# A hybrid decoder layer with expert retrieval: the projections and the convolution done per group of tokens, and two blocks instead of one summed on VectorE

## What is computed

```python
h = rmsnorm(x, norm1_g)
z_glu, q, k, v, qm, gate_logits = jnp.split(h @ w_in, IN_SPLITS, axis=-1)
conv_y = silu(layernorm(depthwise_conv31(a * sigmoid(b)))) @ w_conv_out   # a, b: halves of z_glu
swa_o  = sliding-window attention over blocks of 128; mem_o = attention over 256 memory tokens
merged = g_conv * conv_y + g_swa * (swa_o @ w_swa_out) + g_mem * (mem_o @ w_mem_out)
x = x + merged @ w_out
xb = rmsnorm(x, norm2_g)                  # then, for every block of 128 tokens:
eid, gate = top-16 of 128 x 128 product keys, for each of 8 heads      # 128 experts per token
act = gelu(einsum('td,thkd->thk', xb, w_down[eid]))
x = x + einsum('thk,thkd->td', gate * act, w_up[eid])
```

## Time and profile before

| | |
|---|---|
| time, median of 3 runs | 3336.84 us (3334.49 to 3349.33) |
| span of the profiled execution | 3347.1 us |
| TensorE busy | 3087.0 us, 92% |
| VectorE busy | 2512.8 us, 75% |
| GpSimd busy | 1611.7 us, 48% |
| ScalarE busy | 779.2 us, 23% |
| moved by DMA | 1077.16 MB, mean 322 GB/s |

### The profile page before, as it was taken

How to read it: one execution, slowest core, us unless ns; L and a number is a source line. 1 busy time by engine, 2 the same in 40 slices (tenths; PEclk the granted TensorE clock), 3 DMA queues, 4 the chain that set the end, 5 groups by cost and what they waited for, 6 DMA issues and landing times.

```text
span 3347.1 us, 33154 instructions
## 1 busy us (share of the span) xinstructions
PE 3087.0 (92%) x11349; PEld 1818.7 (54%) x11349; DVE 2512.8 (75%) x5082; ACT 779.2 (23%) x2063; POOL 1611.7 (48%) x1269
## 2 busy tenths in 40 slices
PE   8999798998989999779999999999999999997874
PEld 5677687866847654445545445545545545543321
DVE  2298434986889789888988888888888868455556
ACT  2001542321310114324214204204204214200000
POOL 0000002545145677745566667557657657444434
PEclk9999899999998999899999999999999999998998
DMA  3111466999599999999999999999999999899998
GB/s 130 43 37 58 147 204 231 336 334 354 197 339 351 359 404 397 331 368 370 381 353 388 357 380 388 344 389 385 358 377 380 359 400 373 335 410 393 408 410 316
DMA packets 326171, 1077.16 MB, mean 322 GB/s; under 512 B 40468, under 2 KB 73877, under 8 KB 325340
## 3 DMA queue, kind: packets, MB, share of 16 engines
q0 software_dynamic: 172416, 625.03, 48.7%
q1 hardware_dynamic: 119275, 428.87, 34.1%
q10 hardware_dynamic: 34312, 21.16, 2.0%
HBM read 1052.50 MB, written 23.94 MB: 322 GB/s over the span
## 4 chain that ended last, share of the span: by engine, by line
PE 29%; DMA 20%; DVE 15%; issue 13%; POOL 10%; ACT 1%; ACTq 1%; DVEq 0%; POOLq 0%
PE psum L1666 17%; DMA arena<-in_w_down,arena 12%; POOL arena L1404 9%; DMA arena<-in_w_up,arena 7%; DVE arena L2019 5%; PE psum L1469 4%; PE psum L1642 2%; PE psum L1529 2%; PE psum L1513 1%; ACTq L2264 1%; PE psum L1612 1%; DVE arena L2113 1%; DMA arena<-scratch_s 1%; DMA arena<-in_w_q 1%; PE psum L1515 1%
## 5 line engine op out<-in xcount | busy, mean ns | idle before, releaser
L1404 POOL DMA_INDIRECT arena<-in_w_down,arena x1024 | 1419.2, 1386 | 735.5 <-DVE arena L2019 503.1
L1666 PE MATMUL psum<-arena 128*128 128x512 f32 x3584 | 1602.0, 598 | 77.1 <-DMA arena<-in_w_up 70.8
L2019 DVE CUSTOM_DVE_ANT_0 arena<-arena 128x1024 f32<-128x1024 f32 x1024 | 1220.0, 1222 | 256.3 <-DMA arena<-in_w_down,arena 247.8
L1666 PEld LDWEIGHTS psum<-arena 128*128 128x128 f32 x3584 | 664.4, 191 | 871.0 <-issue 734.3
L1513 PE MATMUL psum<-arena 128*128 128x256 f32 (+2 forms) x1536 | 361.6, 390 | 17.0 <-DVEq L1831 5.5
L2321 ACT ACTIVATE arena<-arena 128x128 f32<-128x128 f32 x896 | 285.6, 390 | 323.8 <-DVE arena L2043 314.7
L2043 DVE TENSOR_TENSOR arena<-constants,arena 128x1024 f32<-128x1024 f32 x224 | 273.4, 1224 | 77.7 <-PE psum L1469 65.0
L1513 PEld LDWEIGHTS psum<-arena 128*128 128x128 f32 x1536 | 267.9, 195 | 99.5 <-issue 13.3
L1469 PEld LDWEIGHTS psum<-arena 128*128 128x128 f32 x1792 | 237.8, 195 | 153.2 <-ACT arena L2321 86.6
L1469 PE MATMUL psum<-arena 128*128 128x128 f32 x1792 | 245.0, 281 | 40.4 <-ACT arena L2321 40.2
L2113 DVE SCALAR_TENSOR_TENSOR arena<-arena 128x1024 f32<-128x1024 f32 x128 | 164.4, 1284 | 122.6 <-DMA arena<-in_w_up,arena 121.3
(11 more groups left out here) (317 smaller groups left out, 2039.8 us busy)
## 6 DMA issues: line engine op xcount, KB each, us to landing
arena<-in_w_up SPq DMA_DIRECT2D x512, 512.0 KB
arena<-in_w_gates SPq DMA_DIRECT2D x96, 768.0 KB
arena<-in_w_o SPq DMA_DIRECT2D x40, 512.0 KB
arena<-in_w_q SPq DMA_DIRECT2D x32, 512.0 KB
arena<-in_w_down,arena POOLq DMA_INDIRECT x1024
arena<-in_w_chunks SPq DMA_DIRECT2D x26, 512.0 KB, 3.5
arena<-scratch_s POOLq DMA_DIRECT2D x64, 128.0 KB
scratch_s<-arena ACTq DMA_DIRECT2D x11, 512.0 KB
```

The costliest lines, as they stand in the source:

```text
L1404: pool.indirect_dma_start(dst, None, table, bass.IndirectOffsetOnAxis(ap=idN[:, min(n, NT - 1) % 2, j:j + 1], axis=0)).then_inc(here, 16)
L1666: mm = pe.matmul(psum[:, 2 * (m % 2) + h, :], coef_block(m, s % NKEYS), wup[s % WUPR][:, h * 512:(h + 1) * 512], start=first, stop=end)
L2019: dve.tensor_tensor_reduce(row, row, rowD[slot_of["x", n]], 1.0, 0.0, ALU.mult, ALU.add, dots[:, n % 3, j:j + 1]).then_inc(row_used, 1)
```

## The change

The first program block now normalises the first 128 columns, then the rest, then the memory, and multiplies nothing but the sums of squares. The 26 chunks become items of the third block, for each group of columns anew, with their weights in the ring of three buffers: per group four "ba" (both halves of the gated unit, two chunks each), four "qq" (queries, two chunks each), one "kv", and once four "mm" (memory, two chunks each). That makes 4 x 9 x 2 + 8 = 80 chunk loads. The convolution is done per group in eight parts on VectorE, the normalisation behind it per group ("ls", "lv"). The planner places all of them. GB = 2 blocks are summed on VectorE, DENSE is 6, so that (6 + 1) x 64 = 448 pieces of w_up are read and 2 x 128 up rows gathered.

```diff
+        FIRST_LOADS = [("b", 0), ("a", 0), ("b", 1)]
...
-        DENSE = NT - 1
+        GB = 2
+        DENSE = NT - GB
...
-        items = att(0) + mixed(pairs_of(0, 0)[0:6], range(1, 6), 1) + pairs_of(0, 0)[6:] + mixed(pairs_of(0, 1, 2), range(6, 10), 4)
...
+        items = glus(0) + [("kv", 0)] + qi[0:2] + [("bu", 0), ("bu", 1)] + mems[0:2] + st[0] + qi[2:3] + st[1] + [("mt",)] + qi[3:4]
+        items += st[2] + [("ls", 0)] + mems[2:3] + st[3] + [("lv", 0)] + mems[3:4] + st[4] + \
+            pairs_of(0, 0)[0:2] + st[5] + pairs_of(0, 0)[2:]
+        items += woven_in(pairs_of(0, 1, 2), {8: glus(1)[0:1], 12: glus(1)[1:2]})
+        for a in (1, 2, 3):
+            bs, qi, qs, st = glus(a), heads_in(a), queries(a - 1), att_steps(a)
+            old_us = group_us[a - 1]
+            items += outs(a - 1, 0) + bs[2:3] + turns(old_us[0:1]) + bs[3:4] + turns(old_us[1:2]) + qs[0:1] + [("kv", a)] + qs[1:4] + scores(old_us)
...
+            items += qi[0:2] + st[0] + qi[2:3] + st[1] + qi[3:4] + st[2] + [("ls", a)] + st[3] + [("lv", a)] + st[4] + st[5]
...
+                items += mixed(pr, st[6:], 1) + woven_in(pairs_of(a, 1, 2), {8: glus(a + 1)[0:1], 12: glus(a + 1)[1:2]})
...
-        rows_at = [48704, 49728, 50752, 11328, 37888] + [25600 + D * i for i in range(4)] + [46144] + [8256 + D * i for i in range(3)] + \
+        rows_at = [48704, 49728, 50752, 33792, 34816] + [25600 + D * i for i in range(4)] + [46144] + [8256 + D * i for i in range(3)] + \
...
-        open_from = [0] * 5 + [184] * 4 + [KEPT] + [122] * 3 + [2] + [80] * 2 + [0] * 2 + [190] * 2
-        open_to = [SLOTS * (NT + 1)] * 3 + [262, 116] + [SLOTS * (NT + 1)] * 5 + [262] * 3 + \
-            [310] + [258] * 2 + [50] * 2 + [238, 258]
+        open_from = [0] * 5 + [350] * 4 + [KEPT] + [310] * 3 + [2] + [80] * 2 + [0] * 2 + [205] * 2
+        open_to = [UPS] + [SLOTS * (NT - 1) + 96] * 2 + [15, 15] + [UPS] * 5 + [370] * 3 + \
+            [390] + [370] * 2 + [50] * 2 + [350, 370]
...
+        accs = [rowD[q] for q in SUM_SLOTS]
...
+            if convs and conv_due <= m.now and all(m.done("glu", item_of("ba", 2 * (convs[0][1] // 4) + c, convs[0][0])) for c in range(2)):
+                m.put("conv", *convs.pop(0))
+                conv_due = m.now + (4.0 if convs and convs[0][0] else 0.0)
+                continue
...
+                    elif it[0] in ("ba", "qq"):
+                        first, n = group_cols(it[2])
+                        for j in range(2):
+                            w = load_here(k, j)
+                            for c in range(KD):
+                                mm = pe.matmul(psum[:, b + j, 0:n], w[:, c, :], hT[:, c, first:first + n],
+                                               start=(c == 0), stop=(c == KD - 1))
+                        mm.then_inc(item_done, 1)
...
                 def up(u):
-                    if u == 0:
-                        dve.wait_ge(coef_done, NT)
-                        dve.wait_ge(x1last_here, 16)
-                    else:
+                    g, j = u // SLOTS, u % SLOTS
+                    if j == 0:
+                        dve.wait_ge(coef_done, DENSE + g + 1)
+                        dve.wait_ge(x1last_here[g], 16)
+                    if u:
                         dve.wait_ge(up_sum, u)
                     row = row_wait(("up", u))
-                    dve.scalar_tensor_tensor(out=acc, in0=row, scalar=dots[:, (NT - 1) % 3, u:u + 1],
-                                             in1=acc if u else x1last, op0=ALU.mult, op1=ALU.add).then_inc(up_sum, 1)
+                    dve.scalar_tensor_tensor(out=accs[g], in0=row, scalar=dots[:, (DENSE + g) % 3, j:j + 1],
+                                             in1=accs[g], op0=ALU.mult, op1=ALU.add).then_inc(up_sum, 1)
...
+                def conv(a, part):
+                    first, n = conv_cols(a)
+                    half, q = part // 4, part % 4
...
+                    for t in range(8 * q, min(8 * q + 8, TAPS)):
+                        for c in (2 * half, 2 * half + 1):
+                            y = yT[:, c, first:first + n]
...
+                                ins = dve.scalar_tensor_tensor(out=y, in0=uT[:, c, t:t + n], scalar=cw[:, c, t:t + 1], in1=y,
+                                                               op0=ALU.mult, op1=ALU.add)
```

More of the change, by code:

```diff
@@ L311, in _ @@
+                mm.then_inc(summed, 1)
+                for k in range(KD):
+                    pe.wait_ge(squared, 2 * KD + k + 1)
+                    mm = pe.matmul(psum[:, 3, 0:MEM], ones, sqm[:, k, :], start=(k == 0), stop=(k == KD - 1))
+                mm.then_inc(summed, 1)
             @block.vector
@@ L448, in build_kernel @@
+        probT = [memN[:, i // 4, (i % 4) * P:(i % 4 + 1) * P] for i in range(8)]
         ck = at(29120, NB, WIN + 1)
@@ L555, in build_kernel, with glus, heads_in, woven_in @@
-        items += pr[4:5] + qs[2:3] + [("xv",)] + qs[3:4] + scores([3, 4]) + pr[5:] + pairs_of(3, 1, 2)[0:12] + [("ids0",)] + pairs_of(3, 1, 2)[12:]
+        def glus(a):
+            return [("ba", c, a) for c in range(NC)]
+        def heads_in(a):
+            return [("qq", i, a) for i in range(NC)]
+        def woven_in(main, extra):
+            out = []
+            for i, it in enumerate(main):
+                out += extra.get(i, []) + [it]
+            return out
+        mems = [("mm", i) for i in range(NC)]
@@ L1075, in build_kernel @@
             if sample_att < 3 and m.landed.get(("load", SAMPLE_LOADS), m.now) + 4.0 <= m.now:
-                ready = [True, m.done("item", items.index(("xs",))), m.end.get(("xmax",), m.now) + 2.5 <= m.now][sample_att]
+                ready = [m.done("copied", last_ao), m.done("item", items.index(("xs",))), m.end.get(("xmax",), m.now) + 2.5 <= m.now][sample_att]
                 if ready:
@@ L1099, in build_kernel @@
                 continue
-            if dot_next == SLOTS * (NT + 1) and not last_put and m.end["up", SLOTS - 1] + 3.0 <= m.now:
-                m.put("last")
-                last_put = True
+            if last_next < GB and m.end.get(("up", SLOTS * last_next + SLOTS - 1), m.now) + 4.0 <= m.now:
+                m.put("last", last_next)
+                last_next += 1
                 continue
@@ L1221, in rec_index @@
             return NX + recs.index(s) + 1
+        tail = [s for s in plan if s[0] in ("snorm", "last") or s in (("norm", DENSE - 2), ("norm", DENSE - 1))]
         row_order = [s for s in plan if s[0] in ("dot", "up")]
```

878 lines of the change are left out of this document (516 added, 362 removed).

## The result

The changed kernel takes 3524.39 us (median of 4 runs, 3519.83 to 3528.24), the kernel before, run beside it, 3342.53 (4 runs, 3334.49 to 3349.33): ratio 1.0537, 95% interval 1.0511 to 1.0563. It is slower by 5.4%. The forecast was 3373 us, slower by 1.1%, with a range up to 3475. The side was right, the size was not: 151 us are missing. (The kernel before was run again beside the experiments, with medians of 3346.76 us beside e1 to e4, 3352.64 beside e5 to e8, 3350.22 beside e9 to e11 and 3347.60 beside e12. A difference between runs of two such groups can carry up to 10 us of that, and where it matters the ratios to the kernel before are compared.)

The account below looks back on a forecast made before the run. A queue of bytes that starts late: dense steps start at 1544 us with 470 gathers done, 692 MB at 380 GB/s take 1821 us, plus 18: 3383 us span, 3373 in the median's terms (+1.1%); range 3250 to 3475.

Parts of the forecast that it names:

- end = T + 2487 - 1.38 R: Whole kernel: end in the profiled span's terms from T and R; the span stood 10 us over the median.
- T: Time at which the dense steps start: 1459 us before, 1544 us forecast, bounds 1474 to 1635.
- R: Number of gathers done by T: 377 before, 470 forecast, bounds 415 and 540.
- The largest term, 60 us of waits for in_w_chunks: Before the dense steps: 40 two-chunk items wait on a ring of three buffers, +60 us, bounds 0 and 121.
- My reading through the planner's tables: Gathers done by T from rows the new table demands: 317 + 80 + 60 = 457.
- the one through VectorE's time: Gathers done by T from VectorE 92% busy between 360 us and T: near 470.
- After T: From the dense steps' start: 692 MB at 380 GB/s take 1821 us, then 18 us to the end.
- TensorE's freed 264 us at nothing: Behind T: TensorE saves 229 us of records and 35 of scatter products, but ends nothing sooner.
- the one on the last gathers: End of kernel: GpSimd issues last gathers 1.32 us apart, under the 1.38 that 0.524 MB take at 380 GB/s.
- Items wait: Rival, slower still: two-chunk items wait 3.02 us each, 3433 us; lone last gathers may add 52 us; chance 0.17.
- lone gathers are slow: Sign of being wrong: DMA share well below 0.95 after T, from this or another bound.
- The rule that spoke against the last step: Last gathers: two-port VectorE instructions lock GpSimd out of writing descriptors, so adds would stretch each gather; the trace doesn't show it.

Follow-up runs that it names:

- e1: The changed kernel with one block, not two, left to fetched up rows, seven multiplied, the group-wise front kept: 3380.21 us, ratio 1.01.
- e4: The changed kernel with eight row buffers, not five, for the last 190 up rows: 3465.15 us (one run).
- e5: The changed kernel with the sample rows' and sixth block's sums behind the last up row and eight row buffers for the last 190: 3418.06 us, ratio 1.0197.
- e8: e5's kernel with the second of every two dense matmuls cut from 512 to 64 columns, loads and fetches kept: 3438.57 us (one run).
- e9: The kernel before with two blocks by fetched rows on its old front, sums last and three more row buffers: 3449.89 us, ratio 1.0296.
- e11: e5's kernel with projection and query weight loads, from the fourth on, fetching only the first half of each piece: 3386.83 us (one run).
- e12: e9 with one constant changed, putting the loads of the two sums 44 pieces later: 3436.33 us, ratio 1.0248.
- e7: e5's kernel with the odd taps of the convolution (15 of 31) left out: 3420.32 us (one run).
- e6: The changed kernel with six row buffers, not five, for the last 190 up rows, order as changed: 3482.68 us (one run).
- e2: The changed kernel with the sample rows' sum and the sixth block's sum placed behind the last up row: 3483.46 us, ratio 1.0405.
- e3: The changed kernel with VectorE's adds cut to 64 of 1024 columns from the 65th up row on, fetches kept: 3467.14 us (one run).

## Why the prediction was right or wrong

In the prediction's terms end = T + 2487 - 1.38 R, less 10. Its sums come out as written. One reading does not: from the eighth slice on three slices of the earlier trace rows are below 90% (one at 5, two at 8), not one; no term rests on it.

- **T**: 1544 forecast, 1579 measured, inside its bounds. +35 us. The chunk products start at 55.9 us instead of 34, as forecast (+21). The largest term, 60 us of waits for in_w_chunks, came out at 26.3 us and was too high. Of the 119 us by which T moved, 22 are TensorE's own work (1347.9 us busy up to T, 1325.4 before; I had put 6 for narrower products) and 97 are idle. In the idle part the waits for VectorE's L1803 grew from 8.3 us (14.2 with 5.9 at the same products put down to L1831) to 27.7, and 14.4 us for ScalarE's L2328 at the attention products (L1603) are new, which I had priced at 10 us or at nothing; the waits for ScalarE's L2534 (22.8 us) were there before (21.8). Halving the loads gave 25 us back (e11).
- **R**: 470 forecast, 459 measured. +15 us. First gather 334 us, forecast 360. My reading through the planner's tables (457) was better than the one through VectorE's time (470): rows done at a given item are a matter of the order, not of a free engine (e7 freed 72 us of VectorE, and R was 460).
- **After T**: with T and R as measured the formula gives 1579 + 2487 - 633 - 10 = 3423 us. e5, the change without its two faults, takes 3418.06. From its first dense step to its last gather it moves at 381 GB/s for 1815 us, 691 MB. So the 692 MB at 380 GB/s, TensorE's freed 264 us at nothing (e8) and the 18 us at the end stood, and the 1.32 us of a lone gather where eight buffers serve the adds (e5's timeline). The close agreement is in part luck: in the terms of the span, without the 10 us, the formula gives 3433 and e5's profiled span is 3410.4. These 50 us of T and R are inside the range.
- **The step that failed** is the one on the last gathers: "GpSimd issues 128 gathers more, but each of the last ones 1.32 us after the one before (1.02 and 0.30 idle)". That pace was read in a burst. In the kernel before nine gathers go out so after 3290 us, while TensorE works on the sample rows' product and waits for no piece; then GpSimd waits for adds again:

```profile
3298.10 1.02 POOL L1404 DMA_INDIRECT arena<-in_w_up,arena  x1 [0.30 <-issue]
3299.43 1.45 POOL L1404 DMA_INDIRECT arena<-in_w_up,arena  x1 [0.30 <-issue]
3301.18 0.94 POOL L1404 DMA_INDIRECT arena<-in_w_up,arena  x1 [0.30 <-issue]
3303.37 0.94 POOL L1404 DMA_INDIRECT arena<-in_w_up,arena  x1 [1.25 <-DVE arena L2113]
3305.77 0.93 POOL L1404 DMA_INDIRECT arena<-in_w_up,arena  x1 [1.46 <-DVE arena L2113]
```

  The burst of the earlier trace rows follows the last pieces and has nine gathers too. Neither shows what a ring of buffers sustains: six sustain 1.43 to 1.47 us (e6), five 1.70. I never costed that the two sums take buffers 1 and 2, though the change names it, and I took the gathers for limited by bytes, 1.38 us each, with the ring at nothing. Eight buffers give 59 us back (e4). The rival "Items wait" had the number, 1.69 us each and 52 us in all, but by another cause, slow issue by itself; e4 excludes it, with issues of 1.02 us beside the same adds.
- **The term that was missing**: the moved sums. The prediction says of no instruction that the planner placed it behind up rows with a wait on a late product; before, the sample's sum was held back until all up rows were added, and the change dropped that condition. Mended alone it gives 41 us back (e2).
- Together the two are worth 106 us (e5), or 114 by the ratios, and 50 + 106 = 156, against 151 missing. That the two agree within 5 us is closer than these measurements can tell, with 10 us between the medians of the kernel before.
- **The signs named**: the DMA share above 0.97 held until 3073 us and then failed (0.73, 0.89), which the prediction named as "lone gathers are slow".

The rule that spoke against the last step, of the Trainium skill (SBUF — State Buffer, "SBUF: two separate sides"), speaks of VectorE instructions in a two-port mode; whether the adds run in one, no run here shows, and the prediction applied it to them without that. With eight buffers and adds back to back the median of an issue is 1.02 us, with short adds 0.94 (e3): 0.08 us, not a lock for the length of an add. In the five-buffer tail issues over 1.5 us are frequent (51 of 151 from 3185 to 3440 us), and they are not with short adds (4 of 190 in e3) nor with eight buffers (10 of 187 in e4 from 3180 us on); why a short ring and wide adds together make them is open.

## What to carry to other kernels

When a tail is left to one queue, count the buffers of its ring before and after the change: here its pace was about the longer of the issue time and the buffer's round over the number of buffers, and a sum parked in a ring buffer is paid for with every transfer. Read a pace where it is sustained, not in a burst that lives on buffers free at its start. Where a planner writes the order, look at each wait placed among the instructions that free buffers: if its producer can be late, put it last, where it costs only itself. Try a change of two parts in all four combinations: here the part that costs 34 us beside one partner costs nothing measurable beside the other.

## What was not expected of the hardware

Indirect gathers of 128 rows of 4 KB went out every 1.27 to 1.32 us where the ring allowed it, 397 to 410 GB/s from one core, both with VectorE at 97% (e4, 1.31 us) and at 22% (e3, 1.27 us). The Trainium skill (DMA: Bandwidth & Descriptors, "Specifications") gives about 358 GB/s as the limit of HBM per core; these windows lie above it, like the 400 GB/s of the kernel before. When the ring was short, the time did not show as waits alone: in the changed kernel GpSimd's visible waits for adds in the last 350 us are 19.1 us, while the issue instructions themselves last 1.32 us on average, where e4's last 1.02 in 3300 to 3380 us. With short adds the same ring of five shows the opposite, 0.97 us per issue and 38.2 us of waits (e3). A profile that shows an engine busy issuing can hide a ring that is too short.
